# One-hot columns from a one-tensor comparison behind the turn, and ScalarE copies inside two norms, in a two-block transformer kernel

## The chip, the cores and the metric

The kernel runs on one core of one Trainium2 chip. The metric is the device time of one execution in microseconds (us). The engines are called PE (TensorE, the matmuls), DVE (VectorE), ACT (ScalarE), POOL (GpSimd) and SP (SyncE, which here only issues loads and stores). Each has a queue of its own, in the order in which the program writes it, and they wait for each other by semaphores.

## The reference, cut to what matters

Two blocks work on 512 tokens of width 1024 in float32: the first mixes them by a short convolution, latent attention and retention; the second has gated linear attention, sparse attention (each token keeps its highest index scores, found by top-k rounds) and attention to a memory, and then a mixture of 16 experts. What the change touches is the norms, for the mean of squares and its inverse root,

```python
def rms_norm(x, w):
    xf = x.astype(jnp.float32)
    y = xf * lax.rsqrt(jnp.mean(xf * xf, axis=-1, keepdims=True) + EPS)
    return (y * w.astype(jnp.float32)).astype(x.dtype)
```

and the dispatch to the experts: each token goes to a few of the 16 experts, its row is multiplied by that expert's weights, and the results are added with the router's weights.

## The kernel before

**Precision.** A float32 product is made of three matmuls of rounded (fp32r) operands: high times high, low times high, high times low (L865 to L867). Activations and weights are therefore kept as a rounded part and a remainder.

**Weights.** They come in units of 128 x 1024 elements. SP loads a unit into one of four `raw` slots (L787). ACT copies it to `w_hi` (`split_high`, L1566), and POOL subtracts to get `w_lo` (`split_low`, L816). For every second unit of the memory's keys and values (`mem_kv`) and for unit 5 of each expert the DVE does the subtraction (L2718, L2728). SP may fill a `raw` slot again only when the remainder in it is done. An expert has six units: up, gate and down.

**Order.** `make_order` writes one list of steps, and each engine walks it and does its share of each step. `("part", name, unit, bank)` are the products of one weight unit into one PSUM bank; before them ACT and POOL prepare units up to three ahead. `spread(a, b)` deals the steps of one list evenly among those of another. ("weights", n) prepares expert units up to n. Where a step stands in the list decides behind what it stands on every engine.

**Norms.** `norm_scale` has ACT square the tiles with a running sum (L1589), the DVE make the mean, ACT the logarithm and the exponential (L1572, L1574, each with a table load), and the DVE finish the inverse root (L2138 to L2142) and scale the tiles (L2156). `mla_sums` does it for the heads of queries and keys: ACT squares nine tiles (L2007). `norm_scale("h2")` stands in the middle of the products of `mem_kv0`; the results of `mem_kv0` to `mem_kv3` are accumulated in banks 0 and 1, and ACT copies them to `mk` and `mv` (L1725), the first of them only after the last tile of `xs` is scaled. `dsa_scale` makes the inverse roots for the sparse attention's keys and its two halves of queries, among products (`dsa_q0`, `dsa_q1`, `gate00`) dealt between the top-k rounds of the DVE (`top_round`, MAX8 L2446 and MATCH_REPLACE8 L2448).

**Dispatch.** `route` gives `hot`, 1 where a token uses an expert. `sort` on PE ranks the tokens of each expert: `before_t` (a triangle of ones) times the tile's own `hot`, and `all_ones` times the tiles before it (L1295, L1297), and counts them (L1301). The DVE turns the ranks into `so` (L2601). Experts go in pairs. For each of the 8 pairs `one_hot` makes `perm` (L2614): four tiles of 128 x 256, a 1 where `iota` is equal to the rank of the token; both inputs of the instruction are SBUF tensors repeated by a stride of 0. PE then gathers the pair's tokens by a product with `perm` (`resort`, L1318), carries their combine weights (L1331) and turns `perm` itself (`permT`, L1341). `most_rows` on the DVE derives from the counts a flag for an overflow path (L2622 to L2626).

**An expert.** `up` makes the hidden products, ACT and DVE activate them (`hid`, L2650), `turn` transposes `hid` on PE (L1364) and the DVE splits it (`hid_hi` L2657, `hid_lo` L2659), `down` multiplies and ACT and DVE split the result into `y_hi` and `y_lo` (L2667). Between these stand jobs: in an odd expert the gathering of the next pair, in an even one (from 2 on) eight `unsort` jobs, each with four products `permT` x `y` (L1389, L1390) in a bank that the DVE then adds to the output `x` (L2675). Four of these jobs stand before `turn` and four behind it. `perm` of the pair after next stands at the end of the odd expert, after its `down`, and so on the DVE before the next expert's `hid`.

## Time and profile before

| what | value |
|---|---|
| three runs | 1562.0, 1564.96, 1573.22 us (median 1564.96) |
| the profiled execution | 1570.75 us, its span 1568.9 us |
| mean granted TensorE clock | 0.96 of full speed |
| PE busy | 1446.6 us (92% of the span), 7130 matmul records |
| DVE, ACT, POOL busy | 719.2, 718.2, 583.5 us |
| subtractions L816 of POOL | 190 of `w_lo`, mean 2.418 us |

The span runs from the first to the last instruction; the execution's own time is 1.85 us longer. All times of the trace count from the span's start, and those of an execution compare with each other, not with the median, unless the difference is stated. A row of the timeline joins equal instructions that follow each other (xN), and in square brackets stands the engine's idle time before it and what ended that. A clock of 1.00 is PE's upper level, 2.4 GHz, and 0.50 its lower, 1.2 GHz. Idle time of an engine that nothing waits for costs nothing.

### The profile page before, as it was taken

The numbers are of one execution on the slowest core, as the hardware profiler recorded it, in microseconds if no ns is written. First come the engines' busy times: TensorE is split into PE (matmuls) and PEld (weight loads), VectorE is DVE, ScalarE is ACT, GpSimd is POOL, SyncE is SP. The second block draws the span as 40 slices with busy tenths as digits, with TensorE's granted clock in tenths as the row PEclk, the third lists the DMA queues.
The fourth block names the chain that finished last, engine by engine and source line by source line (L and its number), as shares of the span: only waits on it lengthen the run. The fifth ranks groups of instructions, "written<-read, shape, count | busy, mean of one in ns | idle before, by whom it ended". The sixth has DMA issues, their size and how long they took to land.

```text
span 1568.9 us, 19085 instructions
## 1 busy us (share of the span) xinstructions
PE 1446.6 (92%) x7130; PEld 1143.8 (73%) x7130; DVE 719.2 (46%) x1460; ACT 718.2 (46%) x1176; POOL 583.5 (37%) x259
## 2 busy tenths in 40 slices
PE   5999888989899998999899999999999698999998
PEld 4777665457677765857778778888887687888886
DVE  2295454444420224247954341324222555666665
ACT  4542325234542646445454764454223354555551
POOL 3265111003253312413422234224434357666662
PEclk9999998889999998999999999999999799999998
DMA  4222111003543211312312123123333046555552
GB/s 147 83 86 69 53 41 35 16 22 108 174 140 92 67 55 41 107 41 68 99 56 61 55 74 108 54 61 97 105 123 98 27 149 188 161 164 173 166 175 90
DMA packets 97860, 146.22 MB, mean 93 GB/s; under 512 B 11854, under 2 KB 46980, under 8 KB 97764
## 3 DMA queue, kind: packets, MB, share of 16 engines
q1 hardware_dynamic: 94672, 140.40, 29.3%
q10 hardware_dynamic: 2804, 4.52, 1.0%
q8 instruction: 60, 0.98, 0.3%
q14 instruction: 36, 0.29, 0.1%
q0 software_dynamic: 288, 0.02, 0.0%
HBM read 140.72 MB, written 4.19 MB: 92 GB/s over the span
## 4 chain that ended last, share of the span: by engine, by line
PE 73%; DVE 16%; ACT 7%; issue 3%; POOL 1%; DMA 1%; SPq 0%; DVEq 0%; ACTq 0%
PE ps L865 16%; PE ps L866 16%; PE ps L867 16%; PE ps L1318 4%; DVE perm L2614 4%; DVE work L2448 2%; DVE best L2446 2%; PE ps L1389 2%; PE ps L1390 1%; PE ps L1003 1%; PE ps L1204 1%; PE ps L1221 1%; PE ps L1177 1%; PE ps L1258 1%; PE ps L1239 1%
## 5 line engine op out<-in xcount | busy, mean ns | idle before, releaser
L816 POOL TENSOR_TENSOR w_lo<-raw,w_hi 128x1024 fp32r<-128x1024 f32 (+2 forms) x190 | 456.7, 2418 | 883.0 <-ACT w_hi L1566 852.4
L1566 ACT ACTIVATE w_hi<-raw 128x1024 fp32r<-128x1024 f32 (+3 forms) x206 | 208.6, 1037 | 124.0 <-PE ps L867 112.3
L865 PE MATMUL ps<-w_hi,act_hi 128*128 128x512 f32 (+1 forms) x560 | 231.7, 414 | 7.5 <-POOL w_lo L816 5.9
L866 PE MATMUL ps<-w_lo,act_hi 128*128 128x512 f32 (+1 forms) x560 | 220.1, 393 | 0.0
L867 PE MATMUL ps<-w_hi,act_lo 128*128 128x512 f32 (+1 forms) x560 | 219.2, 391 | 0.0
L865 PE MATMUL ps<-w_hi,mix_hi 128*128 128x512 f32 x384 | 160.3, 417 | 9.0 <-DVE mix_lo L2182 6.4
L867 PE MATMUL ps<-w_hi,mix_lo 128*128 128x512 f32 x384 | 151.2, 394 | 0.0
L866 PE MATMUL ps<-w_lo,mix_hi 128*128 128x512 f32 x384 | 151.2, 394 | 0.0
L865 PEld LDWEIGHTS ps<-w_hi,act_hi 128*128 128x128 f32 (+1 forms) x560 | 104.6, 187 | 47.8 <-issue 14.2
L867 PEld LDWEIGHTS ps<-w_hi,act_lo 128*128 128x128 f32 (+1 forms) x560 | 104.5, 187 | 25.1
L866 PEld LDWEIGHTS ps<-w_lo,act_hi 128*128 128x128 f32 (+1 forms) x560 | 104.6, 187 | 23.7 <-issue 1.7
L816 POOL TENSOR_TENSOR more_lo<-raw,more_hi 128x1024 fp32r<-128x1024 f32 x40 | 98.2, 2474 | 55.9 <-ACT more_hi L1566 55.8
L865 PE MATMUL ps<-act_hi,w_hi 128*128 128x512 f32 (+4 forms) x280 | 104.5, 375 | 5.4 <-POOL w_lo L816 4.8
L866 PE MATMUL ps<-act_lo,w_hi 128*128 128x512 f32 (+4 forms) x280 | 104.7, 376 | 0.0
L867 PE MATMUL ps<-act_hi,w_lo 128*128 128x512 f32 (+4 forms) x280 | 103.6, 373 | 0.0
L865 PEld LDWEIGHTS ps<-w_hi,mix_hi 128*128 128x128 f32 x384 | 73.1, 190 | 26.5 <-DVE mix_lo L2182 7.2
L866 PEld LDWEIGHTS ps<-w_lo,mix_hi 128*128 128x128 f32 x384 | 73.2, 191 | 16.6 <-issue 1.7
L867 PEld LDWEIGHTS ps<-w_hi,mix_lo 128*128 128x128 f32 x384 | 73.0, 190 | 16.0
L1389 PE MATMUL ps<-y_hi,permT 128*128 128x512 f32 x128 | 54.9, 429 | 21.9 <-DVE x L2675 21.6
L1318 PE MATMUL ps<-perm,xs_hi 128*128 128x256 f32 x256 | 65.2, 293 | 6.7 <-DVE perm L2614 6.7
L2182 DVE SCALAR_TENSOR_TENSOR mix_lo<-ps,gains,mix_hi 128x256 fp32r<-128x256 f32 (+1 forms) x74 | 34.8, 515 | 66.9 <-ACT mix_hi L1734 40.8
L865 PEld LDWEIGHTS ps<-act_hi,w_hi 128*128 128x128 f32 (+2 forms) x280 | 51.9, 186 | 18.3 <-POOL w_lo L816 5.4
(461 smaller groups left out, 2696.8 us busy)
## 6 DMA issues: line engine op xcount, KB each, us to landing
raw<-in_w_in SPq DMA_DIRECT2D x92, 512.0 KB, 3.6
raw<-in_w_gate SPq DMA_DIRECT2D x64, 256.0 KB, 2.8
raw<-in_w_up SPq DMA_DIRECT2D x64, 256.0 KB, 3.1
raw<-in_w_down SPq DMA_DIRECT2D x32, 512.0 KB, 3.8
raw<-in_w_out SPq DMA_DIRECT2D x16, 512.0 KB, 3.7
raw<-in_w_mem_kv SPq DMA_DIRECT2D x16, 512.0 KB, 4.4
raw<-in_w_o_gla SPq DMA_DIRECT2D x8, 512.0 KB, 3.9
raw<-in_w_o_dsa SPq DMA_DIRECT2D x8, 512.0 KB, 3.8
```

The lines of the kernel that those rows point to most:

```text
L816: pool.tensor_tensor(lo[:, 0:a], raw_slot(g)[:, 0:a], hi[:, 0:a].bitcast(F32), ALU.subtract).then_inc(*POOL.done(("w_lo", g)))
L865: pe.matmul(dst, l_hi, r_hi, start=start, stop=False, skip_group_check=skip)
L866: pe.matmul(dst, l_hi, r_lo, start=False, stop=False, skip_group_check=skip)
L867: return pe.matmul(dst, l_lo, r_hi, start=False, stop=stop, skip_group_check=skip)
L1003: pe.matmul(psf[:, at + first:at + N_META + n], q, kT[0:QKH, i, first:N_META + n], start=True, stop=True).then_inc(*PE.done(("S", "mla", j)))
L1318: mm = pe.matmul(ps[:, bank, cols], x[:, t, P * k:P * k + P], perm[:, t, :], start=(t == 0 and x is xs_hi), stop=(t == NT - 1 and x is xs_ ...
L1389: pe.matmul(ps[:, bank, :], turned, y_hi[:, e % 2, cols], start=(e == e0), stop=False)
L1566: nc.scalar.activation(split_slot(g)[0][:, 0:a], raw_slot(g)[:, 0:a], ACTF.Copy).then_inc(*ACT.done(("w_hi", g)))
L2182: return dve.scalar_tensor_tensor(lo, src, gain, hi.bitcast(F32), ALU.mult, ALU.subtract).then_inc(*DVE.done(key))
L2446: dve.max(best8[:, :], acc).then_inc(*DVE.done(("best", t, i)))
L2448: dve.match_replace(acc, best8[:, :], acc, PICKED).then_inc(*DVE.done(("picked", t, i + 1)))
L2614: dve.tensor_tensor(perm[:, t, :].rearrange("p (j n) -> p j n", j=2), iota[:, :].unsqueeze(1).to_broadcast([P, 2, P]), so[:, t, 2 * pair:2 ...
```

## The change

1. `perm` is written by a TENSOR_SCALAR comparison: one SBUF tensor (`iota`) and one scalar per partition (a column of `so`), 128 x 128 each, so 8 instructions for a pair in place of 4, 64 in place of 32.
2. `perm` of pairs 2 to 7 moves from the end of an odd expert to behind `turn` of the even expert that follows.
3. `hot` becomes fp32r, POOL makes rounded copies of `before_t` and `all_ones`, and the ranks take 7 matmuls (one of 64 columns, six of 16) in place of 10 of 16 columns. The counts, `most_rows` and the reading of the flag become a step of their own behind the first `permT`.
4. `resort` waits for `perm` tile by tile in its first column block.
5. ACT copies one unit of `conv_a` inside `mla_sums` and two units of `mem_kv1` inside `norm_scale("h2")`. `mem_kv1` and `mem_kv3` are accumulated in banks 2 and 3.
6. `dsa_scale` of `q0` stands four parts into `dsa_q1`, that of `q1` four parts into `gate00`.

On the DVE, an even expert's surroundings before, in the order of the program (`y_lo` is the end of the odd expert, `x_56` is the output tile):

```order
L2667 SCALAR_TENSOR_TENSOR y_lo<-ps,combine_s,y_hi 128x512 x2
L2614 TENSOR_TENSOR perm<-iota,so 128x256 x4
L2650 TENSOR_TENSOR hid<-ps,e_silu 128x256
L2675 TENSOR_TENSOR x_56<-ps,x_56 128x512 x4
L2657 CAST hid_hi<-ps 128x256
L2659 SCALAR_TENSOR_TENSOR hid_lo<-ps,hid_hi 128x256
L2675 TENSOR_TENSOR x_56<-ps,x_56 128x512 x4
L2728 TENSOR_TENSOR w_lo<-raw,w_hi 128x1024
```

And now, for the same stretch:

```order
L2685 SCALAR_TENSOR_TENSOR y_lo<-ps,combine_s,y_hi 128x512 x2
L2668 TENSOR_TENSOR hid<-ps,e_silu 128x256
L2693 TENSOR_TENSOR x_56<-ps,x_56 128x512 x4
L2675 CAST hid_hi<-ps 128x256
L2677 SCALAR_TENSOR_TENSOR hid_lo<-ps,hid_hi 128x256
L2633 TENSOR_SCALAR perm<-iota,so 128x128 x8
L2693 TENSOR_TENSOR x_56<-ps,x_56 128x512 x4
L2746 TENSOR_TENSOR w_lo<-raw,w_hi 128x1024
```

`perm` has gone from ahead of `hid` to behind `hid_lo`, with the last four additions now behind it.

On PE, the ranks before, between the router's last product and the first gathering product:

```order
L1283 MATMUL ps<-router_w,act_lo 128x20
L1295 MATMUL ps<-hot,before_t 128x16 x2
L1297 MATMUL ps<-hot,all_ones 128x16
L1295 MATMUL ps<-hot,before_t 128x16
L1297 MATMUL ps<-hot,all_ones 128x16 x2
L1295 MATMUL ps<-hot,before_t 128x16
L1297 MATMUL ps<-hot,all_ones 128x16 x3
L1301 MATMUL ps<-hot,all_ones 128x16 x4
L1318 MATMUL ps<-perm,xs_hi 128x256
```

And now:

```order
L1294 MATMUL ps<-router_w,act_lo 128x20
L1303 MATMUL ps<-hot,before_r 128x64
L1307 MATMUL ps<-hot,ones_r 128x16 x6
L1330 MATMUL ps<-perm,xs_hi 128x256
L1330 MATMUL ps<-perm,xs_lo 128x256
L1330 MATMUL ps<-perm,xs_hi 128x256
```

The ranks are 7 matmuls, and the counts are no longer there.

On ACT, the norm h2 before (`x_56` is the input, `ss` the sums), from the squares to the second pair of copies out of the banks:

```order
L1566 ACTIVATE w_hi<-raw 128x1024 x3
L1589 ACTIVATE xs,ss<-x_56 128x1024 x4
L1572 ACT_TABLE_LOAD
L1572 ACTIVATE ss<-ss 128x4
L1574 ACT_TABLE_LOAD
L1574 ACTIVATE ss<-ss 128x4
L1566 ACTIVATE w_hi<-raw 128x1024 x2
L1725 ACTIVATE mk<-ps 128x512 x2
L1566 ACTIVATE w_hi<-raw 128x1024 x4
L1725 ACTIVATE mk<-ps 128x512 x2
```

And now:

```order
L1602 ACTIVATE xs,ss<-x_56 128x1024 x2
L1579 ACTIVATE w_hi<-raw 128x1024
L1602 ACTIVATE xs,ss<-x_56 128x1024 x2
L1579 ACTIVATE w_hi<-raw 128x1024
L1585 ACT_TABLE_LOAD
L1585 ACTIVATE ss<-ss 128x4
L1587 ACT_TABLE_LOAD
L1587 ACTIVATE ss<-ss 128x4
L1740 ACTIVATE mk<-ps 128x512 x2
L1579 ACTIVATE w_hi<-raw 128x1024 x4
L1740 ACTIVATE mk<-ps 128x512 x2
```

Two of the unit copies stand between the squares, ahead of both table loads.

```diff
@@ make_order
-    dense = item("dsa_q0") + [("dsa_prepare", "k"), ("dsa_scale", "q0")] + item("dsa_q1")
-    gates = item("gate00")
-    dense += [("dsa_prepare", "q0"), ("dsa_scale", "q1")] + gates[:12]
+    turns, gates = item("dsa_q1"), item("gate00")
+    dense = item("dsa_q0") + [("dsa_prepare", "k")] + turns[:4] + [("dsa_scale", "q0")] + turns[4:]
+    dense += [("dsa_prepare", "q0")] + gates[:4] + [("dsa_scale", "q1")] + gates[4:12]
...
-    order += [("perm", 1), ("weights", 8)]
+    order += [("counts",), ("perm", 1), ("weights", 8)]
...
+        if e % 2 == 0 and 2 <= e < N_EXP - 2:
+            order += [("perm", pair + 1)]
         order += jobs[at:] + [wanted[3], ("down", e), ("weights", E_UNITS * e + 14)]
-        if e % 2 and e < N_EXP - 3:
-            order += [("perm", pair + 2)]
@@ POOL
                         pool.memset(all_ones[:, :], 1.0).then_inc(*POOL.done(("all_ones",)))
+                        pool.wait_ge(*POOL.after("all_ones"))
+                        pool.tensor_copy(ones_r[:, :], all_ones[:, :]).then_inc(*POOL.done(("ones_r",)))
+                        pool.wait_ge(sort_in, 32)
+                        pool.tensor_copy(before_r[:, :], before_t[:, :]).then_inc(*POOL.done(("before_r",)))
@@ PE: products into bank_at(name, b)
+        def bank_at(name, b):
+
+            return b + 2 if name in ("mem_kv1", "mem_kv3") else b
@@ PE: sort and counts
-                for t in range(NT):
-                    cols = slice(N_EXP * t, N_EXP * (t + 1))
-                    mm = pe.matmul(ps[:, 6, cols], before_t[:, :], hot[:, t, :], start=True, stop=(t == 0), skip_group_check=True)
+                pe.matmul(ps[:, 6, 0:N_EXP * NT], before_r[:, :], hot[:, :, :].rearrange("p t n -> p (t n)"), start=True, stop=False,
+                          skip_group_check=True)
+                for t in range(1, NT):
                     for b in range(t):
-                        mm = pe.matmul(ps[:, 6, cols], all_ones[:, :], hot[:, b, :], start=False, stop=(b == t - 1), skip_group_check=True)
+                        mm = pe.matmul(ps[:, 6, N_EXP * t:N_EXP * (t + 1)], ones_r[:, :], hot[:, b, :], start=False, stop=(b == t - 1),
+                                       skip_group_check=True)
@@ PE: resort
-                for t in range(NT):
-                    pe.wait_ge(*DVE.after("perm", pair, t))
...
+                        if k == 0:
+                            pe.wait_ge(*DVE.after("perm", pair, t))
+                            pe.wait_ge(*(POOL if t < NT - 1 else DVE).after("xs_lo", t))
@@ ACT: norm_scale, mla_sums
+                    if name == "h2" and i % 2:
+                        split_high(first_unit["mem_kv1"] + 1 + i // 2)
...
+                    if i == 5:
+                        split_high(first_unit["conv_a"] + 3)
@@ DVE: one_hot
                 for t in range(NT):
-                    dve.tensor_tensor(perm[:, t, :].rearrange("p (j n) -> p j n", j=2),
-                                      iota[:, :].unsqueeze(1).to_broadcast([P, 2, P]),
-                                      so[:, t, 2 * pair:2 * pair + 2].unsqueeze(2).to_broadcast([P, 2, P]),
-                                      ALU.is_equal).then_inc(*DVE.done(("perm", pair, t)))
+                    for j in range(2):
+                        op = dve.tensor_scalar(perm[:, t, P * j:P * j + P], iota[:, :], so[:, t, 2 * pair + j:2 * pair + j + 1], None,
+                                               ALU.is_equal)
+                    op.then_inc(*DVE.done(("perm", pair, t)))
```

## Rows read from the trace of the kernel before

**Rows 1.** the page, part 4: the chain that ended last, by engine
```profile
PE 73%; DVE 16%; ACT 7%; issue 3%; POOL 1%; DMA 1%; SPq 0%; DVEq 0%; ACTq 0%
```

**Rows 2.** what PE waited for: us in total, times, longest us
```profile
PE ps L1389 <- DVE x L2675: 18.6, 8, 4.8
...
PE ps L865 <- POOL w_lo L816: 10.7, 6, 3.8
...
PE ps L865 <- ACT mk L1725: 5.8, 1, 5.8
...
PE ps L865 <- DVE gate L2261: 2.6, 1, 2.6
```

**Rows 3.** the tile perm: ns min/median/max, first and last start
```profile
L2614 DVE TENSOR_TENSOR perm<-iota,so x32: 415/2592/2628, 1247.0 to 1496.6; 128x256 fp32r<-128x256 f32 x32
```

**Rows 4.** timeline, an even expert: start us, us, what, [idle before <-releaser]
```profile
1340.75 8.01 DVE L2614 TENSOR_TENSOR perm<-iota,so 128x256 fp32r<-128x256 f32 x4
...
1346.01 7.37 POOL L816 TENSOR_TENSOR w_lo<-raw,w_hi 128x1024 fp32r<-128x1024 f32 x3
...
1349.01 2.65 DVE L2675 TENSOR_TENSOR x<-ps,x 128x512 f32<-128x512 f32 x4
...
1349.74 0.50 PE L1389 MATMUL ps<-y_hi,permT 128*128 128x512 f32 x1 [2.55 <-DVE x L2675]
...
1352.02 0.42 DVE L2659 SCALAR_TENSOR_TENSOR hid_lo<-ps,hid_hi 128x256 fp32r<-128x256 f32 x1
```

**Rows 5.** timeline where ik is scaled
```profile
635.04 0.26 DVE L2415 TENSOR_SCALAR ik<-sm,ss 128x64 f32<-128x64 f32 x1
635.21 0.25 DVE L2417 TENSOR_SCALAR ik<-sm,ss 128x64 f32<-128x64 f32 x1
...
635.44 4.82 POOL L816 TENSOR_TENSOR w_lo<-raw,w_hi 128x1024 fp32r<-128x1024 f32 x2 [3.11 <-ACT w_hi L1566]
...
635.54 2.42 DVE L2417 TENSOR_SCALAR ik<-sm,ss 128x64 f32<-128x64 f32 x1
...
637.88 2.44 DVE L2415 TENSOR_SCALAR ik<-sm,ss 128x64 f32<-128x64 f32 x1
```

**Rows 6.** timeline from the ranks to the first resort
```profile
1242.02 1.22 DVE L2597 TENSOR_TENSOR xs_lo<-x,xs_hi 128x1024 fp32r<-128x1024 f32 x1
...
1242.20 1.03 PE L1295 MATMUL ps<-hot,before_t 128*128 128x16 f32 x4 [5.93 <-DVE hot L2574]
...
1246.49 1.87 PE L1301 MATMUL ps<-hot,all_ones 128*128 128x16 f32 x8
...
1246.95 7.87 DVE L2614 TENSOR_TENSOR perm<-iota,so 128x256 fp32r<-128x256 f32 x4
1246.99 10.05 POOL L816 TENSOR_TENSOR w_lo<-raw,w_hi 128x1024 fp32r<-128x1024 f32 x4 [17.99 <-DVE so L2601]
...
1255.07 0.55 PE L1318 MATMUL ps<-perm,xs_hi 128*128 128x256 f32 x1 [6.71 <-DVE perm L2614]
```

**Rows 7.** timeline at the first permT
```profile
1268.09 1.06 PE L1341 MATMUL ps<-ident,perm 128*128 128x128 f32 x8 [1.38 <-DVE flags L2626]
```

**Rows 8.** timeline at the first products of conv_a
```profile
91.88 0.50 PE L865 MATMUL ps<-act_hi,w_hi 128*128 128x512 f32 x1 [2.79 <-POOL w_lo L816]
```

**Rows 9.** timeline at the norm h2
```profile
410.69 4.83 DVE L2156 TENSOR_SCALAR xs<-x,ss 128x1024 f32<-128x1024 f32 x4
...
415.44 1.21 DVE L2718 TENSOR_TENSOR w_lo<-raw,w_hi 128x1024 fp32r<-128x1024 f32 x1
```

**Rows 10.** timeline at the second dsa scale
```profile
776.79 0.80 PE L865 MATMUL ps<-w_hi,act_hi 128*128 128x512 f32 x1 [3.82 <-POOL w_lo L816]
```

**Rows 11.** windows: us, busy us of each engine (instructions), PEclk, DMA share, GB/s
```profile
92.30:95.70 3.40, 3.40 (x10) 2.62 (x9) 3.37 (x3) 0.00 (x0) 3.40 (x2) 0.50 0.51 154
413.20:420.00 6.80, 3.63 (x9) 2.89 (x10) 4.81 (x5) 2.97 (x4) 2.70 (x2) 0.50 0.54 175
770.00:795.00 25.00, 18.61 (x80) 14.83 (x78) 22.14 (x50) 9.32 (x13) 9.43 (x4) 0.86 0.33 95
```

More of the change, by code:

```diff
@@ L506, in program @@
         so = sb("so", [P, NT, N_EXP], SC + 68.625)
-        hot = sb("hot", [P, NT, N_EXP], SC + 68.875)
+        hot = sb("hot", [P, NT, N_EXP], SC + 68.875, F32R)
+        before_r = sb("before_r", [P, P], SC + 40, F32R)
+        ones_r = sb("ones_r", [P, P], SC + 40.5, F32R)
         over = sb("over", [P, NT, N_EXP], SC + 69.125)
@@ L929, in part @@
                     return
+                at_bank = (3 if name == "latent" else 4) if b == "meta" else bank_at(name, b)
                 if u == 0:
-                    claim((3 if name == "latent" else 4) if b == "meta" else b, *item_readers(name, b))
+                    claim(at_bank, *item_readers(name, b))
                 if b == "meta":
@@ L950, in part @@
                             rows = slice(off + P * b, off + P * b + P) if b < NT else slice(0, P)
-                            mm = product(ps[:, b, 0:n], a_hi[:, k, rows], a_lo[:, k, rows], wh[:, j, :], wl[:, j, :],
+                            mm = product(ps[:, at_bank, 0:n], a_hi[:, k, rows], a_lo[:, k, rows], wh[:, j, :], wl[:, j, :],
                                          first, last)
@@ L1289, in sort, with counts @@
                 pe.wait_ge(*DVE.after("hot"))
-                pe.wait_ge(*POOL.after("all_ones"))
-                pe.wait_ge(sort_in, 32)
+                pe.wait_ge(*POOL.after("before_r"))
                 claim(6, (DVE, ("so",)))
-                for t in range(NT):
-                    cols = slice(N_EXP * t, N_EXP * (t + 1))
-                    mm = pe.matmul(ps[:, 6, cols], before_t[:, :], hot[:, t, :], start=True, stop=(t == 0), skip_group_check=True)
+                pe.matmul(ps[:, 6, 0:N_EXP * NT], before_r[:, :], hot[:, :, :].rearrange("p t n -> p (t n)"), start=True, stop=False,
+                          skip_group_check=True)
+                for t in range(1, NT):
                     for b in range(t):
-                        mm = pe.matmul(ps[:, 6, cols], all_ones[:, :], hot[:, b, :], start=False, stop=(b == t - 1), skip_group_check=True)
+                        mm = pe.matmul(ps[:, 6, N_EXP * t:N_EXP * (t + 1)], ones_r[:, :], hot[:, b, :], start=False, stop=(b == t - 1),
+                                       skip_group_check=True)
                 mm.then_inc(*PE.done(("ranks",)))
+            def counts():
                 claim(4, (DVE, ("most",)))
                 for t in range(NT):
-                    mm = pe.matmul(ps[:, 4, 0:N_EXP], all_ones[:, :], hot[:, t, :], start=(t == 0),
+                    mm = pe.matmul(ps[:, 4, 0:N_EXP], ones_r[:, :], hot[:, t, :], start=(t == 0),
                                    stop=(t == NT - 1), skip_group_check=True)
@@ L1305, in resort @@
             def resort(pair, i):
-                if pair == 0 and i == 0:
-                    for t in range(NT):
-                        pe.wait_ge(*(POOL if t < NT - 1 else DVE).after("xs_lo", t))
-                for t in range(NT):
-                    pe.wait_ge(*DVE.after("perm", pair, t))
                 bank = job_bank["resort", pair, i]
@@ L1532, in _ @@
                     combine_sorted(*a)
-                    if a[0] == 0:
-                        active = load_flags(pe, "pe")
+                elif step == "counts":
+                    counts()
+                    active = load_flags(pe, "pe")
                 elif step == "resort":
@@ L1724, in evict @@
                     dst = (mk if n < 2 else mv)[:, b, 512 * (n % 2):512 * (n % 2) + 512]
-                    nc.scalar.activation(dst, ps[:, b, :], ACTF.Copy).then_inc(*ACT.done(("mkv", n, b)))
+                    nc.scalar.activation(dst, ps[:, bank_at(name, b), :], ACTF.Copy).then_inc(*ACT.done(("mkv", n, b)))
             def resort(pair, i):
@@ L2600, in sort @@
                 dve.wait_ge(*DVE.after("hot"))
-                dve.scalar_tensor_tensor(so[:, :, :], ps[:, 6, 0:NT * N_EXP].rearrange("p (t n) -> p t n", n=N_EXP), 1.0, hot[:, :, :],
+                dve.scalar_tensor_tensor(so[:, :, :], ps[:, 6, 0:NT * N_EXP].rearrange("p (t n) -> p t n", n=N_EXP), 1.0,
+                                         hot[:, :, :].bitcast(F32),
                                          ALU.add, ALU.mult).then_inc(*DVE.done(("so",)))
@@ L2908, in _ @@
                     combine_sorted(*a)
-                    if a[0] == 0:
-                        most_rows()
+                elif step == "counts":
+                    most_rows()
                 elif step == "mla_transposes":
```

2 lines of the change are left out of this document (1 added, 1 removed).

## The prediction, made before the changed kernel ran

> **What bounds the kernel now.** The page's chain comes first [rows 1]: TensorE (PE) is 73% of it, so time is to be had only where PE stands still or runs at the lower of its two clock levels. The DVE holds 16%. Then PE's waits [rows 2]: 18.6 us in eight waits for the output additions L2675, 10.7 for the weight remainders of GpSimd (POOL), 5.8 for the copy `mk`. Last, the timelines around each edit.
>
> The reader has to see one effect in `perm`, the one-hot columns. Its 32 instructions last 415 ns at least and 2,592 in the median [rows 3]. In rows 4 four of them take 8.01 us from 1340.75, and POOL subtracts just then (three in 7.37 us from 1346.01): a subtraction and a `perm` instruction alternate. The additions, which read PSUM, run at their own length under the same subtractions (four in 2.65 us). PE pays at 1349.74 with 2.55 us, because `hid` and the additions stand behind `perm`.
>
> **The comparison itself.** 4 instructions of two inputs become 8 of one tensor and a scalar per partition. Does POOL hold these? The nearest rows are `ik` [rows 5]: TENSOR_SCALAR, SBUF to SBUF, the scalar from SBUF. While POOL is free they take 0.25 to 0.26 us and follow each other every 0.17; while its two subtractions run (4.82 us from 635.44) two of them take 2.42 and 2.44. So one SBUF operand was held as well, once per pending subtraction. The Trainium skill ("VectorE: DVE Perf Modes", What auto-detection actually checks) has a single-source operation with source and target in SBUF use both read ports, and "GPSIMD Engine Reference" (8. Key points) names such a mode, beside two SBUF inputs, as what contends with GpSimd. By that rule rows 5 are what must come, and it speaks against this change. What no row shows is a TENSOR_SCALAR written as fp32r, or a comparison under a subtraction. Price of eight columns: free 8 x 0.17 to 0.26, say 1.6 to 2.1 us; held, about 1.2 us and 2.35 for each subtraction pending. I take held, the row that it is nearest to.
>
> **The six moved builds (pairs 2 to 7).** Removed: `perm` ahead of `hid`. Its stall is 4.8 us at its longest, which is the first, and 2.55 at a later one [rows 2, 4]. Added: `perm` behind `hid_lo` and ahead of the last four additions. In rows 4 `hid_lo` ends at 1352.4; without the stall that is about 1349.9. POOL is then in the second of its three subtractions, which end at 1353.4, so I count two holds, to about 1350.8 and 1353.2, and 6 x 0.2 for the rest: 1354.4. The addition that PE needs ends 0.66 later, about 1355.1. PE has three jobs after `turn` before it needs that bank, each of four matmuls at 0.23: from 1348.4 to 1351.2. Stall 3.9 us against 2.55: 5 x 1.35, and 3.9 - 4.8 for the first: **+5.8 us**. If free, `perm` ends at about 1351.9 and the stall is 1.5: -5 x 1.05 - 3.3 = -8.5. Each hold more or less is 2.4 x 6 = 14.4 us. On the DVE four additions, one remainder and two `y_lo` are queued behind `perm`, and `down` waits for the last of these, so nothing is caught up.
>
> **Ranks and the first build.** The ranks are 20 passes of PE (1242.20 to 1246.49) at 0.21 us, the counts 8 more [rows 6]. After: 7 passes, if rounded operands take one pass each as the 512-column products do. 13 passes less are 2.8 us; the DVE's `xs_lo`, which stands before `so`, ends at 1243.24, ahead of the new end at about 1243.8, and takes nothing of it. If a pass of few rounded columns took twice as long, 1.3. `perm(0)` then meets the four subtractions that `so` releases (10.05 us): before 7.87 us, now up to four holds and about 1 us, +2.5. The wait per tile gives PE 6 matmuls at 0.21, 1.3 us, to do while the last tile is built. The counts come back later, 4 passes or 0.7, before a wait of 1.38 for `flags` that stays [rows 7]. Sum -2.8 + 2.5 - 1.3 + 0.7 = **-0.9 us**. If free, PE starts at about 1244.6 and not at 1255.07, and pays 0.3 for the last tile and 0.7 for the counts: -9.5. POOL's two casts of 128 columns stand in the idle time before its four subtractions, which wait for `so`: nothing. The second cast also waits for a load; if that were late, the ranks would be too, as now.
>
> **Norm of the heads.** ACT copies one unit of `conv_a` before the table loads. Now PE waits 2.79 us for its remainder [rows 8], and a stretch of 3.4 us at clock 0.50 follows, where 10 products run and at 0.23 us 16 would [rows 11]: 1.4 us. Copied some 5 us earlier, the remainder is there in time. Gain 2.8 + 1.4 = 4.2; the copy puts the norm back by 1.04 us, and with it the DVE's rope work, on which PE waits later: **-3.2 us**, between -4.2 and -1.
>
> **Norm h2.** PE waits 5.8 us for `mk` [rows 2], since the copies out of banks 0 and 1 wait for scaled `xs`, and one `xs` is held by POOL (four take 4.83, [rows 9]). Clock 0.50 follows for 6.8 us with 9 products [rows 11], whose 3.8 us would be 2.05 at 0.23: 1.8. With other banks the wait is gone. What is late next: unit 1 of `mem_kv1`, whose remainder is the DVE's (L2718) and stands behind the four `xs`. ACT's two copies put these back by 2.1 us, and the hold of some 2.1 goes, so it still ends at 415.44 + 1.21 = 416.7. Unit 0 gives PE 12 products from 410.6, to 413.3: a wait of 3.4, and perhaps 0.5 at the unit after. 5.8 + 1.8 - 3.4 - 0.5 = **-3.7 us**, between -7.5 and -2.
>
> **The dsa scales.** PE waits 3.82 us for `w_lo` at 776.79 [rows 10], and its mean granted clock is 0.86 over these 25 us [rows 11]. That wait goes or shrinks. But the DVE is busy for 22.14 of 25.00 us there with top-k rounds, whose number and place stay, and PE waits behind them for `gate` (2.6 [rows 2]). PE comes there earlier and waits longer: **0**; at worst +2 (a longer wait, more time at half clock), at best -1.8, an idle time of the DVE in those rounds that others can now fill.
>
> **Sum** against the profiled execution, 1570.75 us (span 1568.9 and 1.85 around it): 5.8 - 0.9 - 3.2 - 3.7 + 0 = -2.0 us. That execution is 5.8 us above the median of the three runs, 1564.96; I carry the difference over: 1563.0.
>
> **Rivals.**
> A. POOL doesn't hold the comparison: its result is rounded on writing, and that may keep it at one element at a time. For it: the results of rows 5 were plain f32, and no row shows a rounded one; against it: rows 5 are the same operation in all else. Terms: -8.5 - 9.5 - 3.2 - 3.7 = -24.9, so 1540.1.
> B. Slower: the eight short instructions meet more subtractions than two, as at `perm(0)` where four are pending. The place is ahead of the last four additions of an even expert, the price 14.4 us for each further hold in all six pairs. With three holds the sum is +12.4 (1577.4), with four +26.8 (1591.8), past 1%. It decides from the third pending subtraction on. For it: eight instructions offer more places to be met, and POOL works in runs of three [rows 4]; against: of the three only two lie behind `hid_lo`.
> C. One hold: without the stall POOL's run lies earlier against `perm`. -2.0 - 14.4 = -16.4, so 1548.6.
> D. The norm parts give nothing, since the DVE's next result is what PE meets, and the rest is as forecast: -2.0 + 6.9 = +4.9, so 1569.9.
>
> **How the numbers follow.** Forecast 0.36, A 0.24, B 0.16 (three holds and four by halves), C 0.14, D 0.10. A measurement of this kernel tells about 1%, 15.6 us, from no change. Faster by over 1%: A and half of C, 0.31. Slower: four holds, and a little for a worse meeting, 0.12. The rest, 0.57, is within 1%. The range goes from 1539 (about half of A lies below) to 1581 (three holds and a margin), with 0.1 left out on either side. The likeliest case alone has 1555 to 1572, from the bounds of the norms and the scales.
>
> **What would show it.** Right: of each pair's eight comparisons two last about 2.4 us and six about 0.25; PE waits near 3.9 us for L2675's successor in even experts, and the wait that ended at 1255 is still over 5 us. At the norms: no half clock near 92, and a wait for the DVE's `w_lo` in place of `mk`. Dsa: the wait at 773 gone, that for `gate` longer by as much. A is right if hardly one of the 64 comparisons is above 0.4 us. The forecast is wrong if the holds are not two, if `perm(0)` is over within 3 us of `so`, or if the time leaves 1555 to 1572.

## The result: 1.0% slower, where no change was forecast

| | before | changed |
|---|---|---|
| median of 20 runs, us | 1566.55 | 1586.65 |
| lowest and highest, us | 1561.4 and 1577.76 | 1572.95 and 1590.77 |
| span of the profiled execution, us | 1568.9 | 1585.8 |

The ratio is 1.0101, 95% interval 1.0081 to 1.0122. The forecast was 1563.0, the range 1539 to 1581: the result lies outside, on the side of rival B. The page of the changed kernel: its span, the row of PE and DVE, and the chain by engine [rows 1].

```profile
span 1585.8 us, 19050 instructions
...
PE 1457.3 (92%) x7113; PEld 1151.0 (73%) x7113; DVE 705.0 (44%) x1492; ACT 717.4 (45%) x1176; POOL 578.3 (36%) x261
...
PE 77%; DVE 14%; ACT 6%; issue 3%; DMA 0%; POOL 0%; SPq 0%; DVEq 0%; ACTq 0%
```

PE is busy for 10.7 us longer than before (1446.6), although it has 17 matmul records less (13 passes of the ranks, 4 of the counts). So PE ran slower for a part of the time, and the lower clock has a part in the loss. What PE waited for, as in [rows 2]:

```profile
PE ps L1401 <- DVE x L2693: 26.1, 8, 5.6
...
PE ps L1330 <- DVE perm L2633: 8.9, 2, 5.2
...
PE ps L875 <- POOL w_lo L822: 7.0, 5, 2.0
...
PE ps L875 <- DVE gate L2278: 6.1, 1, 6.1
...
PE ps L875 <- DVE w_lo L2736: 3.2, 1, 3.2
```

The waits for the additions grew from 18.6 to 26.1 us, and their number stayed. `perm`, `w_lo` of the DVE and `gate` are longer or new, POOL's `w_lo` and `mk` shorter or gone. The tile `perm` [rows 3]:

```profile
L2633 DVE TENSOR_SCALAR perm<-iota,so x64: 272/276/2466, 1241.6 to 1518.1; 128x128 fp32r<-128x128 f32 x64
```

Free, a comparison takes 0.276 us, and held up to 2.466. The timeline shows that it is long just while POOL subtracts: POOL holds it. (A held instruction of the DVE lasts until just behind the end of one of POOL's subtractions.) An even expert [rows 4]:

```profile
1386.81 7.07 POOL L822 TENSOR_TENSOR more_lo<-raw,more_hi 128x1024 fp32r<-128x1024 f32 x3 [0.47 <-ACT more_hi L1579]
...
1390.00 0.42 DVE L2677 SCALAR_TENSOR_TENSOR hid_lo<-ps,hid_hi 128x256 fp32r<-128x256 f32 x1
...
1390.34 4.80 DVE L2633 TENSOR_SCALAR perm<-iota,so 128x128 fp32r<-128x128 f32 x8
...
1395.80 0.80 PE L1401 MATMUL ps<-y_hi,permT 128*128 128x512 f32 x1 [3.92 <-DVE x L2693]
```

`perm` starts where `hid_lo` ends, with two of POOL's three subtractions still to come or under way. Eight comparisons take 4.80 us. Two of them are held, the first, which starts in the middle of a subtraction, for 1.33 us, the second for 2.38, and PE waits 3.92 us. In pair 2 the build meets the end of one subtraction more: 0.85, 2.40 and 2.38 us, 6.45 in all. Three windows of the same pair, with the columns of [rows 11]:

```profile
1388.50:1394.30 5.80, 3.37 (x16) 2.43 (x14) 5.55 (x9) 1.27 (x2) 5.38 (x3) 1.00 0.70 221
1394.30:1401.10 6.80, 5.30 (x13) 4.20 (x14) 4.46 (x10) 0.57 (x1) 0.00 (x0) 0.51 0.34 103
1401.10:1429.60 28.50, 28.50 (x170) 25.42 (x169) 11.10 (x21) 17.57 (x27) 18.27 (x8) 1.00 0.51 151
```

The lower clock begins before the wait is over and lasts 6.8 us; PE is busy for 5.30 of them with 13 matmuls, which at the 0.23 us of full clock are 3.0 us. A whole pair of experts in the kernel before, then in the changed one:

```profile
1378.00:1415.30 37.30, 34.73 (x198) 30.20 (x197) 24.26 (x35) 19.55 (x29) 24.45 (x10) 1.00 0.55 171
```

```profile
1390.30:1431.50 41.20, 37.28 (x197) 32.10 (x197) 21.21 (x38) 19.52 (x28) 23.75 (x11) 0.92 0.51 154
```

37.3 us became 41.2. PE's idle time grew from 2.57 to 3.92, by 1.35; the rest, 2.55 us, is in PE's busy time: 34.73 and 37.28 for the same 197 or 198 matmuls, at a mean clock of 1.00 and 0.92.

The ranks and the first build [rows 6]:

```profile
1239.33 0.27 DVE L2591 TENSOR_TENSOR hot<-rt 128x64 fp32r<-128x64 f32 x1
...
1241.36 0.23 DVE L2618 SCALAR_TENSOR_TENSOR so<-ps,hot 128x64 f32<-128x64 f32 x1 [0.66 <-PE ps L1307]
1241.62 10.15 DVE L2633 TENSOR_SCALAR perm<-iota,so 128x128 fp32r<-128x128 f32 x8
1241.66 9.23 POOL L822 TENSOR_TENSOR w_lo<-raw,w_hi 128x1024 fp32r<-128x1024 f32 x4 [14.00 <-DVE so L2618]
...
1246.48 0.55 PE L1330 MATMUL ps<-perm,xs_hi 128*128 128x256 f32 x1 [5.16 <-DVE perm L2633]
...
1251.04 0.58 PE L1330 MATMUL ps<-perm,xs_hi 128*128 128x256 f32 x1 [3.79 <-DVE perm L2633]
```

From `hot` to `so` it is 2.03 us, where it was 4.81. Then `perm(0)` meets four subtractions and takes 10.15 us, and PE waits twice, 5.16 and 3.79. The second build, `perm(1)`, took 1.43 us before. It now starts 0.8 us ahead of POOL's next three subtractions, five comparisons are through by then, and the last three are held:

```profile
1263.74 8.09 DVE L2633 TENSOR_SCALAR perm<-iota,so 128x128 fp32r<-128x128 f32 x8
...
1264.56 7.20 POOL L822 TENSOR_TENSOR more_lo<-raw,more_hi 128x1024 fp32r<-128x1024 f32 x3 [13.66 <-ACT more_hi L1579]
```

At h2 PE's wait is 3.21 us, for the DVE's `w_lo` [rows 9]:

```profile
414.75 0.78 PE L875 MATMUL ps<-w_hi,mem_hi 128*128 128x512 f32 x1 [3.21 <-DVE w_lo L2736]
```

At the second dsa scale the wait for `w_lo` shrank from 3.82 to 1.64 us [rows 10], and the one for `gate` grew from 2.57 to 6.06:

```profile
781.47 0.50 PE L875 MATMUL ps<-w_hi,act_hi 128*128 128x512 f32 x1 [1.64 <-POOL w_lo L822]
...
793.59 0.77 PE L875 MATMUL ps<-w_hi,mix_hi 128*128 128x512 f32 x1 [6.06 <-DVE gate L2278]
```

**Where the time came from.** The start of the same instruction in both traces, changed less before: -3.3 us at the first `cx` (behind the norm of the heads); -4.4 at the end of h2; -3.2 at the first `dk` (1.2 us given back in a stage that the change doesn't touch, where the clock was at 0.50 for 3.4 us longer); -1.4 at the first `gate`, so the dsa scales cost 1.8; -1.3 at the fourth `xs_hi`, the last copy ahead of the dispatch; -0.8 at the third `permT`, so ranks, `perm(0)`, counts and `perm(1)` together cost 0.5; +17.3 at the last `y_lo`, the end of the last expert, and +16.9 at the end of the span. The stage that has the moved builds, from the third `permT` to the last `y_lo`, is 18.1 us longer.

### The profile page after: what moved, and what is told of

It reads as the page before. It is cut to its first block, busy times and chain, and to the rows that moved or that the text cites. A ratio compares the mean times of both kernels' runs of the same rounds, so it can differ in the third digit from the quotient of the medians.

```text
span 1585.8 us, 19050 instructions
## 1 busy us (share of the span) xinstructions
PE 1457.3 (92%) x7113; PEld 1151.0 (73%) x7113; DVE 705.0 (44%) x1492; ACT 717.4 (45%) x1176; POOL 578.3 (36%) x261
## 4 chain that ended last, share of the span: by engine, by line
PE 77%; DVE 14%; ACT 6%; issue 3%; DMA 0%; POOL 0%; SPq 0%; DVEq 0%; ACTq 0%
PE ps L875 18%; PE ps L876 17%; PE ps L877 17%; PE ps L1330 4%; DVE perm L2633 3%; DVE work L2465 2%; DVE best L2463 2%; PE ps L1401 2%; PE ps L1402 1%; PE ps L1014 1%; PE ps L1215 1%; PE ps L1232 1%; PE ps L1188 1%; PE ps L1269 1%; PE ps L1250 1%
## 5 line engine op out<-in xcount | busy, mean ns | idle before, releaser
L1330 PE MATMUL ps<-perm,xs_lo 128*128 128x256 f32 x256 | 64.9, 292 | 0.0
```

What stands on the lines that cost most here:

```text
L1330: mm = pe.matmul(ps[:, bank, cols], x[:, t, P * k:P * k + P], perm[:, t, :], start=(t == 0 and x is xs_hi), stop=(t == NT - 1 and x is xs_ ...
```

## The experiments

Each was measured beside the kernel before, whose median lay between 1566.55 and 1575.26 us at the different times, half a per cent apart. So each run is also read from its trace, in two stages of it: "head" from the fourth copy `xs_hi` to the third `permT` (ranks, `perm(0)`, gathering, `perm(1)`, first expert), "pairs" from there to the last `y_lo`. The numbers are the kernel's less the kernel before's in that stage, in us. A hold is counted where the instruction lasts more than 1.2 us; not counted are the 0.85 us in pair 2 of the changed kernel, 1.12 us in pair 2 of e2, and the 0.6 us of the first comparison in pairs 3 to 7 of e1.

| kernel | ratio (95%) | holds in `perm` of pair 0, 1, 2, each of 3 to 7 | PE's wait in pairs 3 to 7 | clock 0.50 in pairs | head | pairs |
|---|---|---|---|---|---|---|
| before | 1 | 3, 0, 4, 3 | 2.57 | 6.8 | 0 | 0 |
| changed | 1.0101 (1.0081 to 1.0122) | 4, 3, 2, 2 | 3.92 | 37.6 | +0.5 | +18.1 |
| e1 | 0.9811 (0.973 to 0.9892) | 4, 3, 1, 0 | none | 0 | +1.6 | -22.3 |
| e2 | 1.0223 (1.0152 to 1.0294) | 4, 3, 4, 5 | 6.86 | 58.0 | +0.5 | +38.5 |
| e3 | 1.0059 (1.0027 to 1.0091) | 3, 2, 3, 2 | 3.79 | 41.0 | -3.6 | +18.8 |
| e4 | 1.0227 (1.0156 to 1.0298) | 4, 0, 5, 5 | 6.92 | 64.8 | +2.8 | +40.1 |
| e5 | 0.9846 (0.9782 to 0.9909) | 0, 3, 1, 0 | none | 0 | -2.5 | -21.4 |
| e6 | 0.985 (0.9778 to 0.9921) | 4, 0, 1, 0 | none | 0 | +1.7 | -21.7 |
| e7 | 0.9995 (0.9951 to 1.0039) | 3, 0, 4, 3 | 2.57 | 20.5 | +0.1 | +7.7 |
| e8 | 0.9984 (0.9952 to 1.0016) | as before | 2.57 | 10.2 | +0.2 | +2.9 |
| e9 | 0.9795 (0.9742 to 0.9848) | 4, 3, 2, 1 | none | 0 | +0.5 | -22.4 |
| e10 | 0.9838 (0.9785 to 0.9892) | 3, 0, 1, 0 | none | 0 | -0.1 | -22.4 |
| e11 | 0.9769 (0.9723 to 0.9815) | 0, 0, 1, 0 | none | 0 | -10.4 | -21.7 |
| e12 | 0.9756 (0.9708 to 0.9803) | 0, 0, 1, 0 | none | 0 | -11.5 | -21.7 |

**e1_behind_adds: the six builds behind the last additions.**

```diff
+        order += jobs[at:]
         if e % 2 == 0 and 2 <= e < N_EXP - 2:
             order += [("perm", pair + 1)]
-        order += jobs[at:] + [wanted[3], ("down", e), ("weights", E_UNITS * e + 14)]
+        order += [wanted[3], ("down", e), ("weights", E_UNITS * e + 14)]
```

> The changed kernel with the six moved builds of perm placed four additions later, behind the last additions of x and ahead of the DVE's remainder and y_lo. Theory (the place behind hid_lo costs: two holds make PE stand still for 3.9 us, and a stretch at clock 0.50 follows each such stall): POOL has nothing to subtract there (it is idle for 5.9 us from 1353.4 in the trace of before), the eight comparisons take under 2.2 us, no PE wait for an addition is over 0.5 us in the even experts, no half clock behind them; about 17 us less than before and 34 less than the changed kernel: ratio to before 0.986 to 0.992. Rival (perm ahead of the remainder and y_lo only shifts the wait to down): PE waits 1.6 us or more in down for w_lo or y_lo, ratio 0.995 to 1.0.

```profile
1372.34 4.78 POOL L823 TENSOR_TENSOR more_lo<-raw,more_hi 128x1024 fp32r<-128x1024 f32 x2
...
1376.59 1.98 DVE L2634 TENSOR_SCALAR perm<-iota,so 128x128 fp32r<-128x128 f32 x8
...
1378.50 1.21 DVE L2747 TENSOR_TENSOR more_lo<-raw,more_hi 128x1024 fp32r<-128x1024 f32 x1
...
1380.42 2.40 POOL L823 TENSOR_TENSOR w_lo<-raw,w_hi 128x1024 fp32r<-128x1024 f32 x1 [3.30 <-ACT w_hi L1580]
```

But for its first half microsecond the build falls into POOL's pause (1377.1 to 1380.42). It takes 1.98 us. PE doesn't wait in any even expert, no stretch at half clock is left in the pairs, and a pair takes 34.4 us. The rival's wait in `down` didn't come. The place is the cause of the loss, and the kernel before had 22 us to give there. That is more than the expected 17: the ratio is 0.9811, where 0.986 to 0.992 was expected.

**e2_old_place and e4_only_comparison: the comparison of one operand at the old place**, e2 by the diff below in the changed kernel, e4 by nothing but the change's own edit of `one_hot` in the kernel before.

```diff
-        if e % 2 == 0 and 2 <= e < N_EXP - 2:
-            order += [("perm", pair + 1)]
         order += jobs[at:] + [wanted[3], ("down", e), ("weights", E_UNITS * e + 14)]
+        if e % 2 and e < N_EXP - 3:
+            order += [("perm", pair + 2)]
```

> The changed kernel with perm of pairs 2 to 7 back at the end of the odd expert, as eight comparisons. Theory (the place is at fault): three holds as before, a PE wait of about 2.6 us in the even experts, no half clock behind it, ratio to before 0.997 to 1.001. Rival (the form is at fault, eight short instructions meet every pending subtraction): four or five holds, waits of 5 us or more for the additions with half clock behind, ratio 1.01 or more.

> The kernel before with perm built by eight comparisons and nothing else changed. Theory: held like two operands; perm(0) 4 holds where there were 3, +2.5 us; pairs 2 to 7 as before; ratio to before 1.000 to 1.004. Rival A (not held in this form): 32 short builds, 0.985 or less. Rival (more holds each): 1.008 or more.

In both the rival came: the form is at fault too. An old place of e4:

```profile
1397.88 12.37 DVE L2615 TENSOR_SCALAR perm<-iota,so 128x128 fp32r<-128x128 f32 x8
1397.89 4.76 POOL L816 TENSOR_TENSOR w_lo<-raw,w_hi 128x1024 fp32r<-128x1024 f32 x2 [2.70 <-ACT w_hi L1566]
...
1403.12 7.04 POOL L816 TENSOR_TENSOR more_lo<-raw,more_hi 128x1024 fp32r<-128x1024 f32 x3 [0.47 <-ACT more_hi L1566]
...
1411.23 0.79 PE L1389 MATMUL ps<-y_hi,permT 128*128 128x512 f32 x1 [6.93 <-DVE x L2675]
```

Two subtractions and three more run during the build (POOL starts the second row 0.47 us after the first ends), and the eight short instructions are held once by each: five times, 12.37 us, and PE waits 6.93. Four long instructions could be held four times at most, and were three times, since the first of them starts just ahead of a subtraction and runs free (0.42 us). My theory of "held once per pending subtraction" is what happened; I had not drawn its consequence, that the count is capped by the number of instructions, and that twice as many lift the cap. So at the old place the form costs 38 to 40 us (e2 and e4), and the changed kernel's new place takes back about half of that.

**e3_two_operands: the old form at the new place.**

```diff
-                    for j in range(2):
-                        op = dve.tensor_scalar(perm[:, t, P * j:P * j + P], iota[:, :], so[:, t, 2 * pair + j:2 * pair + j + 1], None,
-                                               ALU.is_equal)
-                    op.then_inc(*DVE.done(("perm", pair, t)))
+                    dve.tensor_tensor(perm[:, t, :].rearrange("p (j n) -> p j n", j=2),
+                                      iota[:, :].unsqueeze(1).to_broadcast([P, 2, P]),
+                                      so[:, t, 2 * pair:2 * pair + 2].unsqueeze(2).to_broadcast([P, 2, P]),
+                                      ALU.is_equal).then_inc(*DVE.done(("perm", pair, t)))
```

> The changed kernel with perm built by four comparisons of two SBUF operands, at the new places. Theory (the place is at fault, and one operand is held as two are): two holds a pair, the wait for the additions 3.3 to 3.9 us, half clock behind it, ratio to before 1.005 to 1.011, as the changed kernel. Rival (the form matters): the wait differs from the changed kernel's 3.92 us by more than 1 us either way.

Two holds, PE's wait 3.79 us against 3.92, half clock for 6.8 us behind each (in pair 3 of the changed kernel 3.4): as the theory has it. At a place with two pending subtractions the form doesn't matter. In the head it does: `perm(0)` has three holds in place of four and `perm(1)` two in place of three, 4.1 us less than the changed kernel.

**e9_two_adds: two additions later.**

```diff
+        order += jobs[at:at + 2]
         if e % 2 == 0 and 2 <= e < N_EXP - 2:
             order += [("perm", pair + 1)]
-        order += jobs[at:] + [wanted[3], ("down", e), ("weights", E_UNITS * e + 14)]
+        order += jobs[at + 2:] + [wanted[3], ("down", e), ("weights", E_UNITS * e + 14)]
```

> The changed kernel with the six moved builds two additions later, between the second and the third of the last four. Theory (a hold for each subtraction still pending, and PE's cost is the stall and then the clock behind it): POOL's last subtraction ends about 3.3 us after hid_lo, the two additions take 1.4 and wait for PE's products, so one hold is left, perm takes about 4 us, PE's wait is 1 to 2.5 us in each of five even experts and no half clock stands behind it; 15 to 22 us less than the changed kernel, ratio to before 0.995 to 1.001. Rival (any build ahead of an addition costs the 3.9 us): as the changed kernel, 1.010.

```profile
1409.23 7.12 POOL L823 TENSOR_TENSOR w_lo<-raw,w_hi 128x1024 fp32r<-128x1024 f32 x3 [0.46 <-ACT w_hi L1580]
...
1414.03 3.78 DVE L2634 TENSOR_SCALAR perm<-iota,so 128x128 fp32r<-128x128 f32 x8
...
1417.74 1.27 DVE L2694 TENSOR_TENSOR x<-ps,x 128x512 f32<-128x512 f32 x2
```

One hold, 3.78 us, as expected; but PE doesn't wait at all, where I expected 1 to 2.5 us, and the gain on the changed kernel is 40.5 us in the pairs, not 15 to 22. In the pairs it equals e1 (-22.4 and -22.3). The two additions ahead have given PE its banks, so 3.78 us are covered; 4.80 us ahead of all four (the changed kernel) were not.

**e10_before_behind: the place alone, in the kernel before**, with its four comparisons of two operands.

```diff
-        order += jobs[at:] + [wanted[3], ("down", e), ("weights", E_UNITS * e + 14)]
-        if e % 2 and e < N_EXP - 3:
-            order += [("perm", pair + 2)]
+        order += jobs[at:]
+        if e % 2 == 0 and 2 <= e < N_EXP - 2:
+            order += [("perm", pair + 1)]
+        order += [wanted[3], ("down", e), ("weights", E_UNITS * e + 14)]
```

> The kernel before with nothing changed but the place of perm for pairs 2 to 7: behind the last additions, in its own form of two operands. Theory (the place alone decides, no subtraction is pending there): perm takes 1.4 us, shorter than eight comparisons of one operand (1.98), the six waits of 17.7 us go, ratio to before 0.986 to 0.991. Rival (the one-operand form has a part in the gain of e1): 0.993 or more.

Pairs -22.4, ratio 0.9838, a little better than the expected 0.986: the six waits were 17.7 us, and of the remaining 4.7 at most 3.4 are the clock behind them (6.8 us at 0.50 in the pairs of before); the rest I can't place. The build took 1.80 us in a pair, not 1.4, against 1.98 in e1, and the pairs gain as much as e1's -22.3: the one-operand form has no part in the gain.

**e5_pool_waits and e6_perm1_first: the head.** Both start from e1.

```diff
# e5
-                        pool.wait_ge(*DVE.after("so"))
+                        pool.wait_ge(*DVE.after("perm", 0, NT - 1))
# e6
-    order += [("counts",), ("perm", 1), ("weights", 8)]
+    order += [("perm", 1), ("counts",), ("weights", 8)]
```

> e1_behind_adds, and POOL's first four subtractions for the experts wait for perm(0) in place of so. Theory (each subtraction that is pending holds one comparison): perm(0) takes about 2.0 us where it took 10.15 with four holds, PE's two waits of 5.1 and 3.8 us before the gathering shrink to about 1 together, and POOL ends its four 2 us later with nobody waiting: 7 to 10 us less than e1. Rival (the time comes back where PE needs the weight remainders of the first expert, or as a hold of the routing step behind perm): less than 4 us.

```profile
1240.67 1.66 DVE L2634 TENSOR_SCALAR perm<-iota,so 128x128 fp32r<-128x128 f32 x8
...
1242.41 9.36 POOL L823 TENSOR_TENSOR w_lo<-raw,w_hi 128x1024 fp32r<-128x1024 f32 x4 [15.68 <-DVE rt L2595]
...
1242.79 2.02 DVE L2599 TENSOR_SCALAR rt<-rt 128x4 f32<-128x4 f32 x1 [0.30 <-ACT rt L1999]
...
1244.84 0.17 DVE L2601 TENSOR_REDUCE rt<-rt 128x4 f32<-128x16 f32 x1
...
1245.05 2.09 DVE L2602 TENSOR_TENSOR rt<-rt 128x4 f32<-128x4 f32 x1
...
1247.17 0.18 DVE L2603 RECIPROCAL rt<-rt 128x4 f32<-128x4 f32 x1
...
1249.53 2.27 DVE L2605 COPY combine<-ss 128x4 f32<-128x4 f32 x1
```

`perm(0)` is free (1.66 us), but the four subtractions now meet the routing weights behind it: a TENSOR_SCALAR of 4 elements takes 2.02 us, a TENSOR_TENSOR of 4 2.09, a COPY of 4 2.27, where each takes 0.16 or 0.17 in e12, in which POOL is idle then; TENSOR_REDUCE and RECIPROCAL keep 0.17 and 0.18. `mix_lo` is late by that, and PE waits again:

```profile
1253.53 0.58 PE L1331 MATMUL ps<-perm,xs_hi 128*128 128x256 f32 x1 [3.88 <-DVE mix_lo L2200]
```

The head is 4.0 us better than e1's, less than the 7 to 10 expected: half of it came back, by the hold of the routing step that the rival named.

> e1_behind_adds with perm(1) ahead of the counts. Theory (perm(1) is late by the flag's chain and then meets three subtractions): no or one hold in perm(1), and the 5.5 us that e1 loses against the kernel before between the first permT and the next shrink to 0 to 2: 3 to 5 us less than e1. Rival (the five lost us come from the counts and the flag themselves, which PE now waits for just before the first expert): no change or up to 2 us more, since the flag comes 2 us later.

```profile
1263.46 1.66 DVE L2634 TENSOR_SCALAR perm<-iota,so 128x128 fp32r<-128x128 f32 x8 [0.83 <-PE ps L1354]
...
1265.03 8.03 POOL L823 TENSOR_TENSOR more_lo<-raw,more_hi 128x1024 fp32r<-128x1024 f32 x3 [13.42 <-ACT more_hi L1580]
...
1266.27 0.77 PE L876 MATMUL ps<-w_hi,mix_hi 128*128 128x512 f32 x1 [2.61 <-DVE flags L2645]
```

`perm(1)` has no hold, and still the head is as e1's (+1.7 and +1.6). PE's wait ahead of the first expert doubled, 2.61 for 1.28, and clock 0.50 lasts 6.8 us in this stretch as in e1. The rival was right: the loss was not the held `perm(1)` but the counts and the flag, which PE now does and waits for just ahead of the first expert. Two more traces agree: from the first `permT` to the third e3, with the same wait of 1.28 us but no lower clock there, loses 2.6 us and not 5.5, and e11 and e12, which have the counts elsewhere, lose nothing.

**e7_dsa_only and e8_norms_only**: the kernel before with only these lines of the change (e8 also has `bank_at`).

```diff
# e7
+    dense = item("dsa_q0") + [("dsa_prepare", "k")] + turns[:4] + [("dsa_scale", "q0")] + turns[4:]
+    dense += [("dsa_prepare", "q0")] + gates[:4] + [("dsa_scale", "q1")] + gates[4:12]
# e8
+                    if name == "h2" and i % 2:
+                        split_high(first_unit["mem_kv1"] + 1 + i // 2)
...
+                    if i == 5:
+                        split_high(first_unit["conv_a"] + 3)
```

> The kernel before with the two dsa scales moved and nothing else. Theory (the DVE's top-k rounds set the end, and PE's longer wait for gate costs clock as well): the wait for gate grows from 2.5 to about 6 us, the wait of 3.8 for w_lo goes or shrinks, 1 to 4 us more than before; within the noise of the whole, so it is read from the trace between the first dk and the first gate. Rival (the saved wait is kept): 2 us less or better at the first gate.

Between the first `dk` and the first `gate` e7 loses 1.8 us, as do the seven other kernels that have the moved scales (1.79 to 1.84); e4, e8, e10, e11 and e12, which don't, differ from before by less than 0.05. So the price is 1.8 us. PE's wait for `gate` grew to 4.5 us, not 6, and the one for `w_lo` shrank from 3.8 to 2.6. The whole doesn't show it (0.9995).

> The kernel before with the two norms' copies and the other banks alone. Theory (both act as forecast, each by its own place): 4.5 us less at the first cx, of which 1 to 1.6 are given back at k_sb, and 2.6 less at h2, where PE waits 3.2 us for the DVE's w_lo in place of 5.8 for mk: in all -4 to -7.5, ratio 0.995 to 0.998. Rival (PE's DVE-bound head loops take it all back): 0.

-4.6 us at the first `cx`, all of it kept at the head loops, and -2.7 over h2. The whole is 0.9984, interval 0.9952 to 1.0016: 7.3 us in the trace's two places, hardly more than noise in the medians. The k_sb price that I had charged didn't come.

Both left the experts untouched, and their pairs still are +7.7 and +2.9 us: their wait in pair 2 was 7.4 and 7.2 us, in the trace of before 4.8, and more of their time was at the lower clock. So that trace is a short one in this stage: against e7 and e8 the changed kernel's pairs are longer by 10.4 and 15.2 us, not by 18.1. One of the waits in pairs 3 to 7 of e7, with the same columns as above, and the window behind it:

```profile
1387.55 0.65 PE L1389 MATMUL ps<-y_hi,permT 128*128 128x512 f32 x1 [2.55 <-DVE x L2675]
```

```profile
1387.50:1390.90 3.40, 3.35 (x9) 2.65 (x10) 2.54 (x5) 1.06 (x1) 3.40 (x2) 0.53 0.69 214
```

The wait of 2.55 us was followed by 3.4 us at clock 0.53, and in the trace of before the same wait was not. Of the 15 waits of 2.54 to 2.58 us in before, e7 and e8 a stretch at 0.50 followed 5; of the 20 waits of 3.79 us and more in pairs 3 to 7 of the changed kernel, e2, e3 and e4 it followed every one. The spread of the kernel before, from 1561 to 1578 us, goes with the clock: in the executions beside the experiments those of 1562 us have a mean granted clock of 0.970 to 0.972, those of 1578 us one of 0.957 to 0.959. Whether it is these waits that make the difference isn't shown, since no second execution of it was traced.

**e11 and e12: the best version from all this.** From e1, with the scales of dsa at their old places, and:

```diff
-                        pool.wait_ge(*DVE.after("so"))
+                        pool.wait_ge(*DVE.after("combine"))
...
-    order += [("route", 0), ("sort",), ("weights", 4), ("perm", 0), ("route", 1)]
+    order += [("route", 0), ("sort",), ("weights", 4), ("perm", 0), ("counts",), ("route", 1)]
...
-    order += [("counts",), ("perm", 1), ("weights", 8)]
+    order += [("perm", 1), ("weights", 8)]
```

e12 also has the four comparisons of two operands.

> Built from what the runs showed: perm behind the last additions, the counts and the flag between perm(0) and the routing weights, POOL's first four subtractions waiting for combine, the dsa scales at their old places, the two norms and the rounded ranks as in the changed kernel, perm as eight comparisons of one operand. Theory: against e1 3 us less at the first gate, and the routing free of holds: PE starts the gathering within 3 us of so and has no wait over 1.5 us before the first expert; 8 to 14 us less than e1 in the trace, ratio to before 0.974 to 0.982. Rival (POOL's four come too late for the first expert): PE waits 3 us or more for w_lo in the first up.

> e11 with perm of two SBUF operands, four instructions a pair. Theory (held once per pending subtraction in either form, and four instructions can be held no more than four times; free they are 0.3 to 0.5 us shorter in a pair): 0 to 4 us less than e11. Rival (one operand is better where nothing is pending): e11 is faster by over 2 us.

The page of e12, and its timeline behind `so`:

```profile
span 1526.6 us, 19018 instructions
...
PE 1429.2 (94%) x7113; PEld 1132.3 (74%) x7113; DVE 671.8 (44%) x1460; ACT 718.0 (47%) x1176; POOL 580.9 (38%) x261
```

```profile
1234.25 1.43 DVE L2633 TENSOR_TENSOR perm<-iota,so 128x256 fp32r<-128x256 f32 x4
...
1236.83 0.55 PE L1331 MATMUL ps<-perm,xs_hi 128*128 128x256 f32 x1 [2.02 <-DVE rt L2599]
...
1238.79 9.41 POOL L823 TENSOR_TENSOR w_lo<-raw,w_hi 128x1024 fp32r<-128x1024 f32 x4 [18.49 <-DVE combine L2609]
```

POOL starts when the routing weights are done, nothing of the DVE is held, and PE starts the gathering 2.8 us after `so` (8.4 us in the kernel before). Its subtractions end at 1248.2, in time for the first expert; the rival of e11 didn't come. Not all that was expected of e11 did either: PE still waits 2.25 us ahead of the gathering (no wait over 1.5 was expected), and from the first `dk` to the first `gate` it gains 1.9 us on e1, not 3. Its span is 11.2 us below e1's, inside the 8 to 14. Medians: e11 1536.9, e12 1533.8 us, against 1575.26 of before beside them. Between the two forms the head differs by 1.1 us and the pairs not at all, and the intervals overlap: the form is then free to choose, and two operands are at least no worse.

## Why the prediction was wrong, point by point

- **The comparison is held** (forecast, against A): right. 19 of the 64 last more than 1.2 us in the changed kernel, and one more 0.85. The Trainium skill ("VectorE: DVE Perf Modes", What auto-detection actually checks) gives a single source in SBUF with its target in SBUF the mode that the prediction took to be held. The rows agree, now also for a comparison written as fp32r: 128 elements in 0.276 us free, up to 2.466 held. They don't for every such operation: TENSOR_REDUCE and RECIPROCAL in e5 have one source and their target in SBUF and were not held (0.17 and 0.18 us).
- **Two holds in each moved build, PE's wait 3.9 us**: right for pairs 3 to 7 (4.80 us, 3.92), though only one of the two lasts 2.4 us and the other 1.33. Pair 2 met a part of a third (6.45 us), and the wait was 5.6, not 3.9.
- **The step that failed is the term of +5.8 us for the six moved builds.** It priced a wait by its own length, 3.9 against 2.55, and put the lower clock behind it at nothing. I had charged that clock behind a wait of 2.79 us at `conv_a`, behind one of 5.8 at h2 and as a risk at dsa, where a wait of 3.82 us stood at a clock drop [rows 8, 10, 11], and didn't charge it behind a wait of 3.9 here. Measured: +18.1 us, of which 7.5 are waits (5 x 1.35 and 0.75) and the other 10.6, above the trace of before, the lower clock: 2.55 us in a steady pair, and in the whole stage PE's busy time grew by 10.2 us, from 243.0 to 253.3, with as many matmuls. With it the sum would have been +8.6 and no longer -2.0.
- **The whole miss** is larger than this step. The median is 23.7 us above the forecast. By the traces, 12.3 of them are the moved builds (18.1 for 5.8), 2.5 the two norms as the changed trace has them (-4.4 for -6.9), 1.8 dsa, 1.4 the head (+0.5 for -0.9), and 0.9 the untouched stages. The last 4.7 come from the reference: I took off the 5.8 us by which the profiled execution of before lay above its median, and that of the changed kernel lies 1.1 above its own. With the clock priced and nothing else, the forecast would have been 1573.6, still 13 us too low.
- **Rival B** had the direction, and with three holds a sum of +12.4 where the span shows +16.9, but that nearness is luck: its mechanism was a further hold in all six pairs, and only pair 2 had a part of one (0.85 us). More holds were met at the old place (five in e2 and e4), where the changed kernel no longer builds these columns.
- **Ranks**: right. `hot` to `so` fell by 2.78 us, 2.8 forecast; a rounded pass of few columns takes no longer. `perm(0)` has four holds and 10.15 us, 10.4 forecast.
- **Counts and `perm(1)`**: not seen. I took the build at 1269.64 as free and as staying so. It and POOL's next three subtractions both came about 6 us earlier, but its lead on them, 1.57 us in e4 and e6, shrank to 0.8 by the counts ahead of it, and eight comparisons need 1.6. The held build cost nothing (e6); the counts and the flag's chain ahead of the first expert cost up to 5.5 us. The head's -0.9 came out as +0.5.
- **Heads' norm**: the gain was 4.6 (e8), I kept 3.2 of 4.2; the give-back didn't show in e8 or e1. That the changed trace has -3.3 at the first `cx` is chance: its `k_sb`, ahead of the change, was already 1.2 us late. **Norm h2**: -2.7 against -3.7, with the next wait at 3.21 against 3.4 forecast. The waits were right, and the clock's share too high; 3.4 us at the lower clock are left there, and the 3.8 us of [rows 11] that I took for its nine products are 3.63 in the row.
- **dsa**: +1.8 (e7), inside my 0 to +2 but not the 0 that I took.
- **Rivals C and D** didn't come.

Still open is why a wait of 2.55 us is followed by half clock in some places and executions and not in others; no run isolates that.

## What to carry to other kernels

Price a wait of TensorE with the clock behind it: find in the profile the shortest waits that are followed by a stretch at the lower level and the longest that are not, and look at which side the new wait falls. While POOL works through a queue, a short comparison, scaling or copy of the DVE between SBUF tiles takes as long as one of POOL's instructions, so cutting one into two doubles what can be held; look for POOL's pause in the timeline and put the work there, or let POOL wait until the DVE's short chain is over. And an unchanged stage that differs between two traces by 8 us sets how much a single profile can prove: steady pairs, compared one with one, prove more than the stage.
